# Value products as three rounded products, with the low parts of the probabilities on GpSimd

## The reference

```python
proj = einsum('btd,dp->btp', x, w_in[l])
o_a = chunked attention, relative-position bias, band of 9 chunks of 64 keys
o_b = sliding window of 2 chunks, 4 query heads on 2 key-value heads, rope, a sink per head
o_c = softmax map 1 - lam * softmax map 2, all earlier chunks, rope, RMS norm per head
o_d = attention to the 256 keys an indexer selects (4 query heads, one key and value), rope
mix = concatenate([o_a, o_b, o_c, o_d], axis=-1)
x = layer_norm(ALPHA * x + einsum('btm,md->btd', mix, w_out[l]))
x = layer_norm(ALPHA * x + einsum('btf,fd->btd', square(relu(x @ w_up[l])), w_down[l]))
```

## Time and profile before

| | |
|---|---|
| time, median of 3 runs | 2766.01 us (2765.85 to 2766.18) |
| span of the profiled execution | 2765.6 us |
| PE busy | 2688.9 us, 97% |
| DVE, POOL, ACT busy | 60%, 46%, 36% |
| attention of layer 0, from the first exponential to the last | 285 to 599 us |
| the same in layer 1 | 1654 to 1969 us |

### The profile page before, as it was taken

How to read it: one execution, slowest core, us unless ns; L and a number is a source line. 1 busy time by engine, 2 the same in 40 slices (tenths; PEclk the granted TensorE clock), 3 DMA queues, 4 the chain that set the end, 5 groups by cost and what they waited for, 6 DMA issues and landing times.

```text
span 2765.6 us, 36226 instructions
## 1 busy us (share of the span) xinstructions
PE 2688.9 (97%) x12768; PEld 2102.4 (76%) x12768; DVE 1645.8 (60%) x3330; ACT 998.6 (36%) x2055; POOL 1262.5 (46%) x1170
## 2 busy tenths in 40 slices
PE   8999899999999999999999998999999999999997
PEld 7788467668788888888887875676787888888886
DVE  3787876635534355544959877776364534355448
ACT  2476454442222212222435654443422222212223
POOL 5433700014666556666364346001156566566661
PEclk9999899999999999999999999999999999999999
DMA  5311344523311111101152122355323101111102
GB/s 155 89 46 46 68 91 93 131 105 97 122 33 32 61 62 61 50 17 63 65 138 57 44 74 57 79 109 119 114 89 111 57 27 39 61 62 61 50 20 80
DMA packets 97418, 203.21 MB, mean 73 GB/s; under 512 B 14010, under 2 KB 23162, under 8 KB 96954
## 3 DMA queue, kind: packets, MB, share of 16 engines
q1 hardware_dynamic: 87800, 175.58, 23.5%
q10 hardware_dynamic: 9440, 25.33, 2.5%
HBM read 138.04 MB, written 8.61 MB: 53 GB/s over the span
## 4 chain that ended last, share of the span: by engine, by line
PE 87%; DVE 7%; issue 2%; DMA 2%; ACT 1%; SPq 1%; POOL 0%; ACTq 0%; DVEq 0%; POOLq 0%
PE ps L1276 8%; PE ps L1278 8%; PE ps L1277 8%; PE ps L1158 8%; PE ps L1301 7%; PE ps L1300 7%; PE ps L1302 7%; PE ps L942 4%; PE ps L943 4%; PE ps L944 4%; PE ps L1206 2%; PE ps L1208 2%; PE ps L1207 2%; PE ps L1133 1%; PE ps L1100 1%
## 5 line engine op out<-in xcount | busy, mean ns | idle before, releaser
L900 POOL TENSOR_TENSOR wlo<-wraw,whi 128x512 fp32r<-128x512 f32 (+2 forms) x336 | 444.7, 1324 | 202.1 <-ACT whi L1363 180.2
L898 POOL CAST whi<-wraw 128x512 fp32r<-128x512 f32 (+2 forms) x272 | 183.6, 675 | 740.2 <-DMA wraw<-in_w_out 289.4
L1276 PE MATMUL ps<-xhi,whi 128*128 128x512 f32 x1024 | 406.1, 397 | 0.0
L1278 PE MATMUL ps<-xhi,wlo 128*128 128x512 f32 x1024 | 405.9, 396 | 0.0
L1277 PE MATMUL ps<-xlo,whi 128*128 128x512 f32 x1024 | 405.9, 396 | 0.0
L2064 DVE TENSOR_TENSOR common<-common,ps 128x512 f32<-128x512 f32 x104 | 69.6, 687 | 460.4 <-PE ps L1302 459.9
L1301 PE MATMUL ps<-wlo,op_hi 128*128 128x512 f32 x784 | 311.7, 398 | 0.0
L1300 PE MATMUL ps<-whi,op_hi 128*128 128x512 f32 x784 | 309.5, 395 | 0.0
L1302 PE MATMUL ps<-whi,op_lo 128*128 128x512 f32 x784 | 308.0, 393 | 0.0
L1507 ACT ACTIVATE probT<-ps 128x512 f32<-128x512 f32 (+2 forms) x456 | 205.2, 457 | 240.4 <-PE ps L1142 73.8
L900 POOL TENSOR_TENSOR wlo<-down_raw,whi 128x512 fp32r<-128x512 f32 x168 | 226.2, 1349 | 98.7 <-ACT whi L1363 92.0
(11 more groups left out here) (249 smaller groups left out, 5495.4 us busy)
## 6 DMA issues: line engine op xcount, KB each, us to landing
wraw<-in_w_up SPq DMA_DIRECT2D x144, 256.0 KB, 3.1
down_raw<-in_w_down SPq DMA_DIRECT2D x112, 256.0 KB, 3.6
wraw<-in_w_in SPq DMA_DIRECT2D x80, 256.0 KB, 2.7
slot<-q_part SPq DMA_DIRECT2D x72, 256.0 KB
slot<-k_part SPq DMA_DIRECT2D x72, 256.0 KB
wraw<-in_w_out SPq DMA_DIRECT2D x64, 256.0 KB, 2.8
slot<-q_part SPq DMA_DIRECT2D x48, 128.0 KB
slot<-k_part SPq DMA_DIRECT2D x48, 128.0 KB
```

The source lines that it names most:

```text
L900: nc.gpsimd.tensor_tensor(lo, loaded, hi.bitcast(F32), ALU.subtract).then_inc(S["w_lo"], 1)
L1276: mm(ps[:, b, :], wh, xhi[:, k, tok], start=(k == 0), stop=False)
L1278: last = mm(ps[:, b, :], wl, xhi[:, k, tok], start=False, stop=(k == KT - 1))
```

## The change

In heads A, B and D every step with at least two query tiles (256, 384 or 512 columns; `fine(n)`) takes its value product as three products of rounded parts: 36 + 24 + 40 = 100 steps of a layer. C and all 128-column steps stay as they were.
- ACT takes the exponential of such a step twice from PSUM: once rounded, to `p_hi`, once in full, to `probT`.
- POOL computes `p_lo` = `probT` - `p_hi` in place (`rest`), step by step.
- The values of each head of A, B and D are split once, four steps before the first use: `v_hi` by ACT, `v_lo` by POOL.
- PE multiplies v_hi x p_hi, v_lo x p_hi and, after a wait for `p_lo`, v_hi x p_lo.
- `LAG` goes from 2 to 3 steps. The evacuation of a half moves with it.
- POOL splits two of the four slabs of w_out at steps 208 and 214 and the next after the last value product, since the new tiles lie in the ring's places. The ring starts anew in layer 1, and its first slabs wait for the last user of their place in layer 0.
- POOL's clearings of two slots move into its loop over the steps, two steps later; `junk`, the unused output of the maxima, becomes bfloat16 to make room; some semaphores are shared by both layers.

The core of the diff (the functions that rotate queries and keys are only cut into pieces in it, and run as before, since C isn't among the kinds):

```diff
-    return (l * SLAB_LAST + n) % RING
+    return n % RING
...
-LAG, TURN_LAG = 2, 6
+LAG, TURN_LAG = 3, 6
...
+V_EARLY = 4
+FINE_KINDS = "ABD"
+V_HEADS = [(kind, h) for kind in "CABD" for h in range({"B": 2, "D": 1}.get(kind, H))]
+V_OF = [V_HEADS.index((kind, {"B": h // 2, "D": 0}.get(kind, h))) for kind, h in HEADS]
+V_FIRST = [min(n for n, z in enumerate(STEPS) if V_OF[JOBS[z[0]][0]] == v) for v in range(len(V_HEADS))] + [N_STEPS]
...
+def v_split_at(n):
+    return [v for v in range(len(V_HEADS)) if max(0, V_FIRST[v] - V_EARLY) == n and V_HEADS[v][0] in FINE_KINDS]
...
+def fine(n):
+    job, _, a, b, _, _, _ = STEPS[n]
+    kind = HEADS[JOBS[job][0]][0]
+    return kind in FINE_KINDS and b - a >= (4 if kind == "C" else 2)
...
+WEIGHTS_AT = [N_STEPS - 20 + 6 * j for j in range(2)]
...
+        p_hi = [tensor(f"p_hi{j}", [P, W], F32R, z) for j, z in enumerate(
+            (ring_at + 20 * W + 32, free_d + 2 * SEQ, ring_at + 36 * W, ring_at + 40 * W, compared_at))]
+        junk = [tensor("junk", [P, SEQ], BF16, free_d), tensor("junk_d", [P, SEQ], BF16, place[7])]
...
-                done, value = RELEASE[SLAB_LAST + n - RING]
+                done, value = RELEASE[max(z for z in range(SLAB_LAST) if ring(0, z) == ring(l, n))]
...
+            def values_lo(v):
+                kind, h = V_HEADS[v]
+                raw_v = raw_d[:, :, D_V - D_Q:N_D + 1] if kind == "D" else {"A": v_a, "B": v_b, "C": v_c}[kind][:, :, h, :]
+                pool.wait_ge(S["v_hi"], passed(l, "v_hi") + v_done(v))
+                nc.gpsimd.tensor_tensor(v_lo[v_place(v)][:], raw_v, v_hi[v_place(v)][:].bitcast(F32), ALU.subtract
+                                        ).then_inc(S["v_lo"], 1)
+            def rest(n):
+                job, _, a, b, _, _, _ = STEPS[n]
+                kind, w = HEADS[JOBS[job][0]][0], P * (b - a)
+                pool.wait_ge(S["p_done"], n + 1)
+                nc.gpsimd.tensor_tensor(p_lo[n % 4][:, 0:w], probT[n % 4][:, 0:w], p_hi[p_place(n)][:, 0:w].bitcast(F32),
+                                        ALU.subtract).then_inc(S["p_lo"], 1)
...
+                for n in range(N_STEPS):
+                    for slot, hd in ((0, 2), (1, 3)):
+                        if n == FIRST_STEP[2 * hd + 2] + 2:
+                            clear_keys(n, slot, hd)
+                    for v in v_split_at(n):
+                        values_lo(v)
+                    if fine(n):
+                        rest(n)
+                    if "C" in FINE_KINDS and n == FIRST_STEP[2]:
+                        clear_last_slot(n + 1)
+                    if n in ROPE_B:
+                        call, op = divmod(ROPE_B.index(n), 6)
+                        turn_b(call, [op])
+                    if n in ROPE_D:
+                        call, op = divmod(ROPE_D.index(n), 6)
+                        turn_d(call, [op])
+                    if n in WEIGHTS_AT:
+                        weights(SLAB_OUT + WEIGHTS_AT.index(n))
...
+                if n == SLAB_OUT + len(WEIGHTS_AT):
+                    pool.wait_ge(S["pv_done"], N_STEPS)
...
+                at_q, w = slice(P * (a - 4 * half), P * (b - 4 * half)), P * (b - a)
                 if turn >= 2:
                     pe.wait_ge(S["o_evac"], turn - 1)
-                mm(ps[0:HD + 1, 5 + turn % 2, P * (a - 4 * half):P * (b - 4 * half)], values(kind, h, kt),
-                   probT[n % 4][:, 0:P * (b - a)], start=fresh, stop=end).then_inc(S["pv_done"], 1)
+                if not fine(n):
+                    pe.wait_ge(S["p_done"], n + 1)
+                    mm(ps[0:HD + 1, 5 + turn % 2, at_q], values(kind, h, kt), probT[n % 4][:, 0:w], start=fresh, stop=end
+                       ).then_inc(S["pv_done"], 1)
+                    return
+                v = V_OF[hd]
+                hi, lo = v_hi[v_place(v)][:, kt, :], v_lo[v_place(v)][:, kt, :]
+                pe.wait_ge(S["v_lo"], passed(l, "v_lo") + v_done(v))
+                pe.wait_ge(S["p_hi"], passed(l, "p_hi") + fine_done(n))
+                mm(ps[0:HD + 1, 5 + turn % 2, at_q], hi, p_hi[p_place(n)][:, 0:w], start=fresh, stop=False)
+                mm(ps[0:HD + 1, 5 + turn % 2, at_q], lo, p_hi[p_place(n)][:, 0:w], start=False, stop=False)
+                pe.wait_ge(S["p_lo"], passed(l, "p_lo") + fine_done(n))
+                mm(ps[0:HD + 1, 5 + turn % 2, at_q], hi, p_lo[n % 4][:, 0:w], start=False, stop=end).then_inc(S["pv_done"], 1)
...
+                    kind = HEADS[JOBS[job][0]][0]
+                    nc.scalar.activation(p_hi[p_place(n)][:, 0:P * (b - a)], ps[:, 2 + n % 2, 0:P * (b - a)], ACT.Exp,
+                                         scale=SCALE[kind]).then_inc(S["p_hi"], 1)
...
+            def values_hi(v):
+                kind, h = V_HEADS[v]
+                raw_v = raw_d[:, :, D_V - D_Q:N_D + 1] if kind == "D" else {"A": v_a, "B": v_b, "C": v_c}[kind][:, :, h, :]
+                if v == 1:
+                    act.wait_ge(S["m_ready"], 3)
+                if v >= 2:
+                    act.wait_ge(S["pv_done"], V_FIRST[v - 1])
+                nc.scalar.activation(v_hi[v_place(v)][:], raw_v, ACT.Copy).then_inc(S["v_hi"], 1)
```

More of the change, by code:

```diff
@@ L473, in build @@
     with ExitStack() as ctx:
[L474 to L479, removed]
+        sem_names = """w_hi w_hi_act w_lo w_used t_ready t_hi t_lo p_ready p_out i_rope i_turned i_ready i_relu i_acc roped qk_ready
+            s_ready s_max m_ready m_turned m_copied m_row st_ready p_done pv_done o_evac o_turned o_out es_ready ones_set
+            masks_ready pool_chain pool_roped mix_done o_ready o_sum x_loaded gb_loaded ln_done u_ready u_relu u_square
+            h_sum u_hi u_lo d_ready d_sum halves misc_loaded chain k_candidate k_counted qk_hi qk_lo ik_hi ik_lo i_stacked""".split()
         sems = [{n: ctx.enter_context(nc.semaphore(f"{n}_{l}")) for n in sem_names} for l in range(DEPTH)]
+        for n in PER_LAYER:
+            sems[0][n] = sems[1][n] = ctx.enter_context(nc.semaphore(n))
         for l in range(DEPTH):
@@ L519, in build @@
         r += 16 * SEQ
+        bias_at = r
         bias_a = tensor("bias_a", [P, H, 2 * P], F32, r)
@@ L527, in build @@
         r += 4 * P + 256
-        probT = [tensor(f"probT{j}", [P, W], F32, r + 4 * W * j) for j in range(3)]
-        probT.append(tensor("probT3", [P, W], F32))
+        prob_at = [r + 4 * W * j for j in range(3)] + [region(4 * W)]
+        probT = [tensor(f"probT{j}", [P, W], F32, prob_at[j]) for j in range(4)]
+        p_lo = [tensor(f"p_lo{j}", [P, W], F32R, prob_at[j]) for j in range(4)]
         assert r + 12 * W <= R1 + 8 * D_MODEL * TILES
@@ L832, in fill, with turn @@
                 then(nc.gpsimd.memset(dst.bitcast(F32), value))
-            def turn(v, heads, cs, half, t0, nt):
+            def turn(v, heads, cs, half, t0, nt, ops=range(6)):
                 v = v.rearrange("p t (h s d) -> p t h s d", s=2, d=half)
@@ L848, in beside_attention @@
-            def beside_attention():
+                if 0 in ops:
+                    then(nc.gpsimd.tensor_tensor(u, b, sin, ALU.mult))
+                if 1 in ops:
+                    then(nc.gpsimd.tensor_tensor(w, a, sin, ALU.mult))
+                if 2 in ops:
+                    then(nc.gpsimd.tensor_tensor(a, a, cos, ALU.mult))
+                if 3 in ops:
+                    then(nc.gpsimd.tensor_tensor(b, b, cos, ALU.mult))
+                if 4 in ops:
+                    then(nc.gpsimd.tensor_tensor(a, a, u, ALU.subtract))
@@ new lines, in turn, with turn_b @@
+                if 5 in ops:
+                    then(nc.gpsimd.tensor_tensor(b, b, w, ALU.add))
+            def turn_b(call, ops=range(6)):
+                if call < 2:
+                    turn(block(B_Q, BLK, 4 * call, 4), 4, cs64, HD // 2, 4 * call, 4, ops)
+                else:
+                    turn(block(B_K, P), 2, cs64, HD // 2, 0, TILES, ops)
+                if call == 2 and 5 in ops:
+                    nc.gpsimd.memset(zero_p[:], 0.0).then_inc(S["pool_roped"], 1)
+                    pool.wait_ge(S["pool_roped"], 2)
@@ new lines, in turn_d, with quiet @@
+            def turn_d(call, ops=range(6)):
+                turn(raw_d[:, 2 * call:2 * call + 2, 0:5 * HD], 5, cs64, HD // 2, 2 * call, 2, ops)
+                if call == 3 and 5 in ops:
+                    nc.gpsimd.memset(zero_p[:], 0.0).then_inc(S["pool_roped"], 1)
+                    pool.wait_ge(S["pool_roped"], 3)
+            def quiet(n):
+                if fine_done(n - 1):
+                    pool.wait_ge(S["p_lo"], passed(l, "p_lo") + fine_done(n - 1))
+                v = max([v for z in range(n) for v in v_split_at(z)], default=-1)
+                if v >= 0:
+                    pool.wait_ge(S["v_lo"], passed(l, "v_lo") + v_done(v))
@@ L850, in beside_attention @@
+            def beside_attention(weights):
                 pool.wait_ge(S["w_lo"], STACK_SLAB)
@@ L858, in beside_attention @@
                 pool.wait_ge(S["pool_roped"], 1)
[L859 to L875, removed]
```

(19 more changed lines are left out.)

61 lines of the change are left out of this document (44 added, 17 removed).

## The result

The changed kernel takes 2774.69 us in the median of 13 runs, 2766.18 the kernel before in 13 runs beside it; ratio 1.0027, interval 1.0019 to 1.0035. It is slower by 8.5 us in the medians, and by 5 to 10 us by the interval; 11 us faster was forecast, and the time lies outside the range of 2745 to 2765. The profiled execution has a span of 2774.6 us, 9.0 above that of before.

What follows compares the result with a forecast made beforehand. PE was taken as the limit in A and D, but not in B. A -3.1, B +1.0 and D -3.5 gave -5.6 us a layer, -11.2 for both: 2754.8 us, range 2745 to 2765.

Steps and rivals of the forecast that it cites:

- The prices of the products: Wide value products on PE: three rounded ones cost 0.70, 0.53, 0.36 us instead of 0.86, 0.65, 0.43.
- 27 by the lower bound: PE's saving for two layers at 0.215 us per 512-column product, against 22.6 us at the prices used.
- D: Attention of heads D: -5.4 us from products, +1.6 for ACT, +0.3 for DVE, so -3.5 us a layer.
- The charge for ACT's boundaries: Stalls of PE behind moved row maximums: 1.6 us a layer in D, 0.7 in A.
- ScalarE's second exponential: One more exponential per wide step, 0.598, 0.491 or 0.383 us; no throughput limit, but stalls at some row maximums.
- The stall of half a microsecond at a row maximum: Scores after a moved row maximum wait about 0.5 us for their bank: one such boundary in A, three in D.
- The lag step: Third lag step moves the 0.59 us evacuation behind the next exponential, offsetting the second exponential's boundary cost in B.
- What POOL does to DVE: POOL's low parts hold DVE's SBUF-only operations, 9 us more DVE work in A, mostly absorbed: charge 0.4 us there.
- B: Attention of heads B: DVE's delays cost 1.0 us a layer and PE's 1.7 us aren't earned, so +1.0.
- (b): Rival: DVE behind POOL's lock bounds B and half of A; 4 us faster, 2762; chance 0.12.
- (c): Rival: score-bank handoff sets the pace; slower, about 2783 at 0.2 us stall a wide step, 2773 at 0.15; chance 0.09.
- Low parts in time: Third value product: PE arrives 4 to 5 us after the wide score, POOL's low part needs 2.8; no wait.

Runs made afterwards that it cites:

- e1: Kernel before with LAG 3 in place of 2, nothing else; 2773.63 us against 2767.53, ratio 1.0020.
- e4: Changed kernel without POOL's low parts of the probabilities, the third product taking the rounded ones again; 2758.87 us, ratio 0.9970.
- e8: Kernel of e4 with one exponential in a wide step, the rounded one, in place of two; 2765.79 us, ratio 0.9987.
- e9: Kernel before, LAG 2, with the evacuation of a finished half one step later; 2765.59 us against 2766.51, ratio 0.9998.
- e10: Kernel before with LAG 3, but the evacuation at the step where it stood with LAG 2; 2774.17 us, ratio 1.0026.
- e3: Changed kernel with DVE's inverse square root for C's norm moved from A's last job to B's last job; 2766.46 us, ratio 0.9999.
- e11: Changed kernel with LAG 3 in A, B and D only, 2 in C, and C's inverse square root at B's end; 2763.54 us, ratio 0.9990.
- e2: Changed kernel with D alone in the rounded form, LAG 3 kept; 2763.22 us, ratio 0.9986.
- e6: Changed kernel with D alone rounded and LAG 2; 2762.71 us, ratio 0.9980.
- e7: Changed kernel with D alone rounded, LAG 3 in D's steps only and 2 in C, A and B; 2758.41 us, ratio 0.9964.
- e5: Kernel of e3 with LAG back at 2; 2784.04 us, ratio 1.0053.

## Why the prediction was wrong, by its steps

- **The prices of the products** were right: 0.70, 0.52 and 0.36 us measured for 0.70, 0.53 and 0.36. (The "27 by the lower bound" lowers only the 512-column steps; with all widths at three quarters of the old price it would be 31. The forecast doesn't use it.)
- **D** was right in sign and too cautious: -5.3 us a layer at the first exponential (-5.7 as cut above), not -3.5. The charge for ACT's boundaries, 1.6 us, isn't there: PE waits in D for maxima alone, 0.7 us in three waits. The value products' 5.4 us account for the gain; e1 would let one expect 0.5 to 1.5 more from the lag step, and where that went isn't shown.
- **ScalarE's second exponential** was over-charged. The stall of half a microsecond at a row maximum was derived from one example. D has no such wait, and A is as long with one exponential as with two, in kernels without the low parts (e4, e8).
- **The lag step** is the first step that failed. The prediction priced it only by what waits for it, a half's evacuation, and credited it in B. It moves every value product of C and A as well, and in the sum C "doesn't change". Measured are +6 us for the step alone (e1), without the evacuation having part in it (e9, e10): 1.7 us a layer in A and 1.2 to 1.4 in four jobs of C, all at full clock.
- **What POOL does to DVE** is the second step that failed, by its size, and it decided. The mechanism was there with its rows, 1.28 us for 0.34, the operations were counted, 30 in A, and 9 us more for DVE were forecast. DVE's busy time in A grew by 7.2 us. But the cost was put at 0.4 us since DVE would have 11 us to spare in A (56 of 67). The spare time was a sum over the stretch; twelve of the thirty operations form one chain in one job, with an output that PE needs queued behind them. There 3.60 us of waiting came at once, in each of the layers. Moving the chain gives 8 us back (e3), and leaving the low parts out gives 16 (e4).
- **B** was forecast at +1.0 us. Layer 1 has -0.3, layer 0 +4.0 at a mean clock of 0.92. The clock there dropped after waits of PE; in e4 layer 0's B also ran at 0.93 and 46.4 us without POOL's low parts, in e11 at 1.00 and 43.4 with them. So it isn't the low parts that make B long. The traces show one thing more: B's clock is 1.00 in both layers of every kernel whose B isn't rounded (before, e1, e2, e6, e7, e9, e10), and below it, 0.92 to 0.97, in 8 of the 12 Bs of the kernels where it is (changed, e3, e4, e5, e8, e11). Why in one layer and not in the other stays open.
- **The rivals.** (b), DVE behind POOL's lock, names the mechanism but lets it come out as 2762; (c) gives the sign, and its 2773 at 0.15 us a step is near the measured time, but by luck: it comes from the bank handoff, which the runs don't show. None had the lag.
- **Low parts in time** held with the third step (3.1 us of waits in all), and the slabs of w_out cost nothing visible: the stretch between the two layers' attention is 1054.9 us for 1055.0.

## What to carry to other kernels

When an engine is given new work whose operations can hold up those of another, as POOL's do with DVE's here (1.20 us for 0.19), look in the other engine's queue for chains of short dependent operations and for what stands queued behind them; the spare time of the stretch says nothing about them. When a pipeline gets one more step of lag, list what it moves, and past which waits, in every part of the program that shares the order, and give the step only to the part that needs it: here D alone, 2758.4 us. And price a change by part: the same edit earned over 5 us a layer in D, where PE waited for almost nothing, and lost in A, where DVE's outputs stood in PE's way.

## What the runs showed that I had not expected

- A DVE operation on 32 columns, 0.19 us alone, took 1.17 us beside POOL's value split (1.20 us) and 1.20 beside a low part of 512 columns (1.27 us). In the other direction, POOL's operations stretched as well: three low parts of 512, 384 and 256 columns, 2.90 us at 478.18 above, took 5.32 in the chain at A's second job boundary, while DVE scanned 896 columns there in 2.72 us (2.02 before). From the chain of waits, kernel after (start us, us added, line):

```profile
440.29 1.96 POOL v_lo L966
442.25 5.32 POOL p_lo L974 x3
```

- In the changed kernel a single wait of PE of 3.60 us was followed by a granted clock of 0.50, with 512-column products 0.42 us apart instead of 0.23.
